# Expert weights of a one-core MoE decoder step: four ring slots per transfer of the first weight (rows of 32 KB), two per transfer of the second (rows of 16 KB)

## The reference, cut to what matters

```python
def run_block(args):
    e, idx = args
    xb = x_pad[idx]
    gu = xb @ w_e1[e] + b_e1[e]          # w_e1[e]: 1024 x 2048
    g, u = gu[:, :D_EXPERT], gu[:, D_EXPERT:]
    g = jnp.minimum(g, SWIGLU_LIMIT)
    u = jnp.clip(u, -SWIGLU_LIMIT, SWIGLU_LIMIT)
    h = (u + 1.0) * (g * jax.nn.sigmoid(SWIGLU_ALPHA * g))
    return h @ w_e2[e] + b_e2[e]          # w_e2[e]: 1024 x 1024
```

## Time and profile before

| | us |
|---|---|
| median of 3 timed runs | 1271.91 (1271.19 to 1272.47) |
| the profiled execution | 1270.08 |
| span of its trace | 1267.8 |
| TensorE busy in the span | 1165.9 |
| mean granted share of the TensorE clock | 0.979 |

### The profile page before, as it was taken

One profiled execution on the slowest core, in us unless ns is written; L12 is line 12 of the kernel. 1 busy time (PEld: TensorE's weight loads), 2 busy tenths in 40 slices (PEclk: granted clock), 3 DMA queues, 4 the chain that ended last, 5 costly groups with the idle time before them and its releaser, 6 DMA issues.

```text
span 1267.8 us, 15137 instructions
## 1 busy us (share of the span) xinstructions
PE 1165.9 (92%) x5540; PEld 567.2 (45%) x5540; DVE 338.3 (27%) x820; ACT 182.1 (14%) x354; POOL 27.7 (2%) x54
## 2 busy tenths in 40 slices
PE   8999999698899999999989898989999999999896
PEld 6888888386333343333333333323332323233332
DVE  3795424614122122021212121211202021212123
ACT  3114213203010111111010101111010111010102
POOL 4000001100000000000000000000000000000000
PEclk9999999888999999999999999999999999999999
DMA  9398333993799999999999999999999999999994
GB/s 302 91 289 274 137 102 132 362 419 115 278 390 416 421 422 422 421 422 422 421 422 422 421 422 422 421 422 421 421 421 422 420 422 422 421 422 422 421 422 168
DMA packets 92741, 457.40 MB, mean 361 GB/s; under 512 B 7827, under 2 KB 36715, under 8 KB 44069
## 3 DMA queue, kind: packets, MB, share of 16 engines
q1 hardware_dynamic: 90768, 452.27, 88.8%
q10 hardware_dynamic: 1117, 3.04, 0.6%
q0 software_dynamic: 832, 1.76, 0.5%
HBM read 453.71 MB, written 3.81 MB: 361 GB/s over the span
## 4 chain that ended last, share of the span: by engine, by line
PE 51%; DMA 24%; SPq 14%; DVE 6%; issue 3%; ACT 2%; ACTq 0%; POOL 0%; DVEq 0%
DMA ring<-in_w_e 23%; PE ps L1539 15%; SPq L353 12%; PE ps L1559 12%; PE ps L1250 11%; PE ps L1269 3%; DVE ring L955 2%; PE ps L1501 1%; PE ps L1510 1%; PE ps L1549 1%; SPq L361 1%; PE ps L1453 1%; DVE mix L1106 1%; DVE mix L1109 1%; DVE mix L1103 1%
## 5 line engine op out<-in xcount | busy, mean ns | idle before, releaser
L1539 PE MATMUL ps<-ring,mix 128*64 128x512 f32 x2016 | 457.5, 598 | 28.9 <-DMA ring<-in_w_e 27.6
L1539 PEld LDWEIGHTS ps<-ring,mix 128*64 128x64 f32 x2016 | 134.1, 136 | 336.8 <-issue 234.8
L1559 PE MATMUL ps<-ring,mix 128*64 128x512 f32 x1024 | 235.1, 613 | 22.0 <-issue 11.0
L1103 DVE TENSOR_SCALAR mix<-ps 128x512 f32<-128x512 f32 x32 | 22.1, 692 | 606.7 <-PE ps L1539 606.7
L1559 PEld LDWEIGHTS ps<-ring,mix 128*64 128x64 f32 x1024 | 79.5, 140 | 156.0 <-issue 142.0
L686 ACT ACTIVATE mix<-mix 128x512 f32<-128x512 f32 x32 | 20.1, 630 | 420.3 <-DVE mix L1103 420.3
L1510 PEld LDWEIGHTS ps<-mix 128*128 128x128 f32 x544 | 65.5, 198 | 14.4 <-issue 13.0
L1510 PE MATMUL ps<-mix 128*128 128x128 f32 x544 | 70.1, 284 | 1.3 <-ACT rstd L668 1.3
L696 ACT ACTIVATE mix<-ps 64x512 f32<-64x512 f32 x64 | 37.8, 591 | 227.1 <-PE ps L1559 226.8
L1090 DVE SCALAR_TENSOR_TENSOR mix<-mix,gates 128x1024 f32<-128x1024 f32 x16 | 20.5, 1284 | 154.8 <-ACT mix L696 154.8
L1250 PE MATMUL ps<-mix,ring 128*128 128x264 f32 x256 | 60.2, 400 | 0.3 <-ACT mix L639 0.3
(11 more groups left out here) (294 smaller groups left out, 651.6 us busy)
## 6 DMA issues: line engine op xcount, KB each, us to landing
ring<-in_w_e SPq DMA_DIRECT2D x380, 1024.0 KB, 25.0
ring<-in_w_in SPq DMA_DIRECT2D x8, 1024.0 KB, 15.7
ring<-in_cache_mem_k SPq DMA_DIRECT2D x8, 1024.0 KB, 4.9
ring<-in_cache_mem_v SPq DMA_DIRECT2D x8, 1024.0 KB, 8.3
ring<-in_w_k SPq DMA_DIRECT2D x4, 1024.0 KB, 8.9
ring<-in_w_v SPq DMA_DIRECT2D x4, 1024.0 KB, 12.7
ring<-in_w_out SPq DMA_DIRECT2D x4, 1024.0 KB, 12.5
ring<-in_w_q SPq DMA_DIRECT2D x4, 1024.0 KB, 12.0
```

The costliest lines, as they stand in the source:

```text
L1103: dve.tensor_scalar(g1, ps[0][:, :], LIMIT, None, ALU.min).then_inc(S["g_clamped"], 1)
L1539: m = pe.matmul(ps[gu][CAP * i:CAP * i + CAP, :], xeT[:, k, CAP * e2:CAP * e2 + CAP], g_u[gu][:, 512 * i:512 * i + 512], start=False, stop ...
L1559: m = pe.matmul(ps[3][CAP * i:CAP * i + CAP, :], hTv[:, k % 4, CAP * (k // 4):CAP * (k // 4) + CAP], ring[:, s, D * (k % 2) + 512 * i:D * ...
```

## The change

A transfer now covers several slots. The first weight is loaded by two transfers of 4 MB (slots 0 to 3 and slots 4 to 7), in each of which every partition gets four neighbouring rows of `w_e1`, 32 KB in one piece. The second weight is loaded by two transfers of 2 MB (slots 8 and 9, slots 10 and 11), with four neighbouring rows of `w_e2`, 16 KB, in each partition. A transfer waits until all of its slots are free, and TensorE's waits are for the whole transfer. As the rows are now dealt to the slots by fours, the columns of `xnt` and `hh` that belong to a slot are every fourth one (`DEAL`), and the `head` loads take every fourth row, too.

```diff
+SPAN = {0: 4, 4: 4, 8: 2, 10: 2}
+DEAL = [slice(4 * P * (_k // 4) + _k % 4, 4 * P * (_k // 4 + 1), 4) for _k in range(KD)]
...
                 sp.wait_ge(S["freed"], free)
                 if s < W_SLOTS:
-                    src = a["w_e1"][0][bass.ds(e, 1), s * P:(s + 1) * P, :].rearrange("o p c -> p (o c)")
-                    dst = ring[:, s, :]
+                    src = a["w_e1"][0][bass.ds(e, 1), s * P:(s + 4) * P, :].rearrange("o (p t) c -> p (o t c)", t=4)
                 else:
                     j = s - W_SLOTS
-                    src = a["w_e2"][0][bass.ds(e, 1), j * 2 * P:(j + 1) * 2 * P, :].rearrange(
-                        "o (p t) c -> p (o t c)", t=2)
-                    dst = ring[:, s, :]
+                    src = a["w_e2"][0][bass.ds(e, 1), j * 2 * P:(j + 2) * 2 * P, :].rearrange(
+                        "o (p t) c -> p (o t c)", t=4)
+                dst = ring[:, s:s + SPAN[s], :].rearrange("p s c -> p (s c)")
                 sp.dma_start(dst, src).then_inc(filled[s], 16)
...
-                for s in range(first, RING):
-                    fill(e, s, RING * b + freed_after(MOE0 + s - RING))
+                for s in SPAN:
+                    if s >= first:
+                        fill(e, s, RING * b + freed_after(MOE0 + s + SPAN[s] - 1 - RING))
...
-                    sp.dma_start(head[k][gu], a["w_e1"][0, 0, k * P:(k + 1) * P, D * gu:D * gu + D]).then_inc(S["head_filled"], 16)
+                    sp.dma_start(head[k][gu], a["w_e1"][0, 0, DEAL[k], D * gu:D * gu + D]).then_inc(S["head_filled"], 16)
...
-            for s in range(HEAD_SLOTS, W_SLOTS):
-                fill(1, s, freed_after(MOE0 + 2 * (s - HEAD_SLOTS)))
+            fill(1, HEAD_SLOTS, freed_after(MOE0 + 2 * (HEAD_SLOTS - 1)))
...
-                            m = pe.matmul(ps[4 + i][:, P * (k % 4):P * (k % 4) + P], xnt[:, t, k * P:(k + 1) * P],
+                            m = pe.matmul(ps[4 + i][:, P * (k % 4):P * (k % 4) + P], xnt[:, t, DEAL[k]],
...
-                        pe.wait_ge(filled[k], 16 * b + 16 * (fills_before(MOE0 + k) - 1))
+                        pe.wait_ge(filled[0], 16 * b + 16 * (fills_before(MOE0) - 1))
                     else:
-                        pe.wait_ge(filled[k], 16 * b + 16 * fills_before(MOE0 + k))
+                        pe.wait_ge(filled[HEAD_SLOTS], 16 * b + 16 * fills_before(MOE0 + HEAD_SLOTS))
...
-                    c = 2 * P * (j // 2) + j % 2
-                    m = pe.transpose(ps[2][:, j * P:(j + 1) * P], hh[:, c:c + 2 * P - 1:2], ident[:, :])
+                    m = pe.transpose(ps[2][:, j * P:(j + 1) * P], hh[:, j:4 * P:4], ident[:, :])
...
-                    if k % 2 == 0:
+                    if k % 4 == 0:
                         pe.wait_ge(filled[s], 16 * b + 16 * fills_before(MOE0 + s))
```

More of the change, by code:

```diff
@@ L373, in _ @@
             fill_head(2)
-            for s in range(HEAD_SLOTS, W_SLOTS):
-                fill(0, s, freed_after(MOE0 + s - RING))
+            fill(0, HEAD_SLOTS, freed_after(MOE0 + W_SLOTS - 1 - RING))
             bias(0)
[L377 to L380, removed]
+            fill(1, 0, freed_after(MOE0 + HEAD_SLOTS - 1 - RING))
+            for s in range(W_SLOTS, RING, 2):
+                fill(0, s, freed_after(MOE0 + s + 1 - RING))
             sp.wait_ge(S["tm_turned"], 6)
@@ L1602, in _ @@
             for k in range(KD):
-                m = pe.transpose(ps[2][:, NB * k:NB * k + NB], xnt[0:NB, 2, k * P:(k + 1) * P], ident[0:NB, 0:NB])
+                m = pe.transpose(ps[2][:, NB * k:NB * k + NB], xnt[0:NB, 2, DEAL[k]], ident[0:NB, 0:NB])
             m.then_inc(S["smp_chain"], 1)
```

## The result

| | before | changed |
|---|---|---|
| median, us | 1270.44 (7 runs, 1269.91 to 1272.47) | 1275.72 (7 runs, 1272.63 to 1278.08) |
| ratio | | 1.0036, 95% interval 1.0024 to 1.0047 |
| span of the profiled execution, us | 1267.8 | 1270.3 |

What follows compares the result with a forecast made beforehand. The weight loads, at 422 GB/s in a full queue, were taken to bound the kernel, not TensorE. Losses of 5.3 us (start) and 5.3 (end) less 7.5 (rate) made +3.1: 1271.91 to 1275.0 us, range 1263 to 1283.

Steps and rivals of the forecast that it cites:

- What bounds the kernel: Expert stage: experts run at the pace of the loads, 59.90 us a pair, TensorE idle some 4.4 us of it.
- the start: Expert 3's first load waits for four slots of expert 2 instead of one: a loss of 5.3 us.
- The end: After expert 31's last first-weight landing, three more slots of 1.75 us before `down`: a loss of 5.3 us.
- all four have to be taken after it: Expert 31: slots 4 to 7 land together when slot 7 lands now, so TensorE takes three slots more afterwards, 5.3 us.
- The rate: Loads from 378.7 to 1239.4 us, 344 slots: fewer rows and completions gain 0 to 24 us, taken as 7.5.
- I take a quarter, 26 ns: Price of a completion in the rate term: a quarter of 105 ns, saving 20 or 13 ns a slot.
- The contiguous, long rows are the near ones, so 0.7 ns: Price of a row in the rate term, from 4 against 8 KB rows: saves 4.5 or 3 ns a slot.
- What else is edited: nothing: Gather's weight loads stepping over four columns cost nothing, since a step of two showed 204 ns against 198.
- The bound next to it, 60 ns: Gather: even 60 ns more on 32 weight loads a pair, 1.9 us, would lie in TensorE's idle time.
- the 4.4 us of cover: TensorE's idle time for each pair of experts, taken to hide any slower weight loads of the gather.
- case 3: Rival: faster, 13 us of gain or more, sign a rate over 428 GB/s; chance 0.27.
- case 1: The forecast: rate rises 0.6 to 1.4% (5 to 12 us), time 1270.5 to 1277.5 us; chance 0.40.

Runs made afterwards that it cites:

- fine_start: deal_at_write with first weights of experts 2 to 6 in two-slot transfers, expert 3's slots 0 to 3 in single slots; 1259.19 us, ratio 0.9909.
- deal_at_write: The changed kernel, but ScalarE deals the columns when writing xnt, so the gather's weight loads read neighbouring columns; 1264.65 us, ratio 0.9948 to before.
- fine_end: deal_at_write with slots 4 to 7 of the last expert in four one-slot transfers, a wait each; 1264.47 us, ratio 0.9942 to before.
- long_transfers_short_rows: The changed kernel's transfers and waits, but the rows (8 KB), layout and gather of the kernel before; 1280.56 us, ratio 1.0081 to before.

## Why the prediction was right, and where it was not

**What bounds the kernel, and the start: right.** The three slots of 1.75 us at expert 3 were predicted from a table of releases. With 8 KB rows and the gather of before, start and end together cost 10.4 us for 10.6 (8.5 to 11.9 by the interval), the dip of the rate there is the predicted 5.3 us later, and fine_start takes back 5.5 of 5.3 by the medians. These agree better than the spread of the runs warrants, as TensorE's own times before expert 2 differ by 2 us and more from trace to trace.

**The end: right in size, incomplete in its mechanism.** Between the last landing and `down` lie 11.5 us in deal_at_write where the prediction had 11.6. But the step "all four have to be taken after it" is true of each lump, and the prediction priced only the last. TensorE is held by the lump before almost as long, and splitting the last one (fine_end) gave 0.2 us, not 5.3.

**The rate: the term was mis-sized, 7.5 us for 15.9.** That is deal_at_write against long_transfers_short_rows, two kernels with the same transfers and different rows. Their traces agree: from the first load of expert 3 to the landing of expert 31's slot 7 a slot takes 2.450 us ((1228.3 - 385.5) / 344) and 2.498 us ((1241.5 - 382.1) / 344), 16.6 us on 344 slots; 385.5 and 382.1 are the start of expert 2 plus 7.0 for four slots and 1.5 for the first bytes, as in the prediction. Both parts of the working failed. "I take a quarter, 26 ns" for a completion: it costs nothing that shows. "The contiguous, long rows are the near ones, so 0.7 ns": from 8 to 16 KB a slot goes from 2.485 to 2.450 us, 8.7 ns for each of four rows, and on to 32 KB (2.433 at 431 GB/s) 8.5 ns for each of two; rates rounded to 1 GB/s leave these two figures open by some 1.5 and 4 ns. That is near the 10.7 of the step from 1 to 4 KB and not near the step from 4 to 8. Why the 4 KB stretch goes as fast as 8 KB rows is open: it is a load of another tensor beside a second queue's packets, and no run here had 4 KB rows in the ring. The slower 404 GB/s of the head loads was then hardly the completions either; no run separates its cause.

**"What else is edited: nothing": wrong, 11.1 us by the medians.** The step that failed is the extrapolation from a step of two to a step of four. The bound next to it, 60 ns, was too small (130), and its cover was read from the steady part. In the start, where the queue is dry, TensorE's time is the release of the slots and has no cover; and in the steady part the 4.4 us of cover shrank to 3.3 as the loads became faster, of which the gather takes 2.7, so that TensorE catches up with the loads only at 1146.7, its first wait. The traces show 6.4 us at the start and 2.4 at the end (deal_at_write), and 8.6 and 1.9 on the kernel before.

The rate gave 8.4 us more than forecast and the gather took 11.1 that weren't forecast. Three steps lead from before to the changed kernel: +10.4 for the lumps, -15.9 for the rows, +11.1 for the gather, together +5.6. That this meets the measured 5.3 checks nothing: each step is the difference of two neighbouring medians, so the sum is the last median less the first. What the experiments show is the size of each. The prediction's figure was good by luck: its two errors had opposite signs, and each of them is larger than the forecast itself. Of the signs listed, two spoke. The rate, 430, lay outside the forecast's 422 to 428 and was case 3 by that sign, while the time was that of case 1. And the rate dipped after 390 us (52 GB/s in the slice from 392), where the last dry spell should have ended near 384: that was the gather.

The Trainium skill (DMA: Bandwidth & Descriptors, Measured) has the rate rise from 341 GB/s at 1 MB to 425 at 16 MB, for transfers issued from GpSimd. Here, issued from SyncE into a queue that is never empty, transfers of 1 MB and of 4 MB with the same rows both go at 422, so the trace doesn't show that rise. The same page's ceiling of 435 GB/s (Where 436 GB/s comes from) isn't reached by any run; the highest mean from 400 to 1180 us is 430.

## What to carry to other kernels

With a full queue, lengthen the rows, and not the transfers: here rows of 16 KB in transfers of two slots had most of the rate (428 GB/s) and a third of the loss at the end (1.7 us), and dealing the columns once where they are written cost nothing that shows. A layout change that helps the loads ends up in someone's operand: look at each reader's row for exactly the step that the change makes, and where the queue is dry count TensorE's work in full. Coarser transfers cost at the start by their release and at the end by TensorE's lag, which only many experts work off.

## What the runs showed of the hardware that I had not expected

A weight load of 128 columns in float32 in the gather takes 196 to 198 ns with a step of one, 202 with two and 328 with four, and its matmul 284, 290 and 402.

In transfers of the same sizes, rows of 32 and 16 KB (two parts and one) arrive at 430 GB/s and rows of 8 KB at 422, 2% apart.

The 32 matmuls of a `down` took 7.1 us in most places, and 8.8 where the granted clock was lower: 0.88 from 1236 to 1250 us in deal_at_write and in fine_end, against 1.00 in the changed kernel. That is 1.7 us on the path at the end, a third of the loss that is looked for there.

The time that SyncE spends on the issue of a transfer fell from a median of 1.92 us to 0.33 us (line 354, 700 to 1180 us, of the changed kernel), though the transfers are larger; the loads land 18.1 us after it:

```profile
L354 SPq DMA_DIRECT2D ring<-in_w_e x66: 332/333/337, 700.0 to 1173.9; - x66
...
DMA to landing us min/median/max: 12.9/18.1/22.1
```
